# Opening of the first sequence: norm statistics from the transposed x

## The reference, cut to what matters

```python
mod = jnp.dot(jax.nn.silu(c), w_ada) + b_ada
shift1, scale1, gate1, shift2, scale2, gate2 = [m[:, None, :] for m in jnp.split(mod, N_MOD, axis=-1)]

h = (_rmsnorm(x, g_mix) * (1.0 + scale1) + shift1).astype(dt)   # x * rsqrt(mean(x*x, -1) + EPS) * g
proj = jnp.einsum('bsd,de->bse', h, w_in)
q, k, v, g_sw, p, gate_a, gate_b = jnp.split(proj, IN_SPLITS, axis=-1)
...
log_g_f = jax.nn.log_sigmoid(ret_decay_f.astype(jnp.float32))   # decay constants of the retention
log_g_b = jax.nn.log_sigmoid(ret_decay_b.astype(jnp.float32))
```

## Time and profile before

| | |
|---|---|
| median of 3 runs | 2575.28 us (2574.32 to 2575.88) |
| the profiled execution's own time | 2576.01 us |
| its span, first to last instruction | 2574.2 us |
| TensorE busy | 2517.1 us, 98% |
| VectorE, ScalarE, POOL busy | 71%, 46%, 68% |
| read from HBM | 284.36 MB |

### The profile page before, as it was taken

How to read it: one execution, slowest core, us unless ns; L and a number is a source line. 1 busy time by engine, 2 the same in 40 slices (tenths; PEclk the granted TensorE clock), 3 DMA queues, 4 the chain that set the end, 5 groups by cost and what they waited for, 6 DMA issues and landing times.

```text
span 2574.2 us, 34798 instructions
## 1 busy us (share of the span) xinstructions
PE 2517.1 (98%) x12684; PEld 2106.4 (82%) x12684; DVE 1820.2 (71%) x2182; ACT 1176.8 (46%) x1818; POOL 1741.0 (68%) x1165
## 2 busy tenths in 40 slices
PE   6999999999999999999999999999999999999998
PEld 3889898978778888878888888888777888888886
DVE  4978888877886666765859797978678555555434
ACT  5433333335654545555634333333456554555443
POOL 1777777757287777655656969696655877775545
PEclk9999999999999999999999999999999999999998
DMA  9124242446055355497631424241541323325764
GB/s 332 42 84 136 84 136 84 152 178 211 25 164 177 129 172 172 160 347 226 191 117 42 158 62 156 64 157 52 187 123 53 115 86 115 107 88 193 210 193 147
DMA packets 296009, 362.15 MB, mean 141 GB/s; under 512 B 17312, under 2 KB 178464, under 8 KB 295840
## 3 DMA queue, kind: packets, MB, share of 16 engines
q1 hardware_dynamic: 292960, 349.44, 42.0%
q10 hardware_dynamic: 2880, 10.49, 1.1%
HBM read 284.36 MB, written 75.50 MB: 140 GB/s over the span
## 4 chain that ended last, share of the span: by engine, by line
PE 82%; DVE 10%; ACT 2%; issue 2%; DMA 1%; POOL 1%; SPq 1%; DVEq 0%; POOLq 0%; ACTq 0%
PE ps L1099 27%; PE ps L1265 15%; PE ps L1529 13%; PE ps L1461 9%; PE ps L1160 5%; PE ps L1480 3%; PE ps L1370 3%; DVE state L2890 1%; PE ps L1548 1%; PE ps L1583 1%; DVE qdT L2871 1%; PE ps L1197 1%; PE ps L1314 1%; PE ps L1559 1%; DVE late_rows L2698 1%
## 5 line engine op out<-in xcount | busy, mean ns | idle before, releaser
L2276 POOL TENSOR_TENSOR f_w<-f_ring,f_w 128x512 fp32r<-128x512 f32 x434 | 595.3, 1378 | 397.2 <-ACT f_w L1857 392.2
L1099 PE MATMUL ps<-hc_hi,f_w 128*128 128x512 f32 x2240 | 690.4, 389 | 3.5 <-ACT u_act L1931 2.9
L2215 POOL TENSOR_TENSOR f_w<-f_ring,f_w 128x512 fp32r<-128x512 f32 x282 | 468.1, 1674 | 202.2 <-ACT f_w L1650 201.8
L1099 PEld LDWEIGHTS ps<-hc_hi,f_w 128*128 128x128 f32 x2240 | 420.0, 188 | 92.9 <-ACT u_act L1931 3.7
L1099 PE MATMUL ps<-hc_lo,f_w 128*128 128x512 f32 x1120 | 435.8, 389 | 0.0
L1265 PE MATMUL ps<-act_ring,f_w 128*128 128x512 f32 x1848 | 421.4, 390 | 2.7 <-ACT f_w L1857 1.4
L1265 PEld LDWEIGHTS ps<-act_ring,f_w 128*128 128x128 f32 x1848 | 346.5, 188 | 76.6 <-issue 3.2
L1857 ACT ACTIVATE f_w<-f_ring 128x512 fp32r<-128x512 f32 x434 | 269.8, 623 | 250.8 <-POOL f_ring L2286 109.5
L1529 PE MATMUL ps<-hb,f_w 128*128 128x512 f32 x1440 | 347.4, 395 | 0.0
L1650 ACT ACTIVATE f_w<-f_ring 128x512 fp32r<-128x512 f32 x282 | 176.0, 627 | 356.0 <-POOL f_ring L2223 186.7
L1529 PEld LDWEIGHTS ps<-hb,f_w 128*128 128x128 f32 x1440 | 268.3, 188 | 61.3 <-issue 6.7
(11 more groups left out here) (262 smaller groups left out, 4047.4 us busy)
## 6 DMA issues: line engine op xcount, KB each, us to landing
f_ring<-in_w_in SPq DMA_DIRECT2D x176, 256.0 KB, 4.3
f_ring<-in_w_up SPq DMA_DIRECT2D x160, 256.0 KB, 3.4
f_ring<-gated_out SPq DMA_DIRECT2D x154, 256.0 KB, 3.1
late_rows<-in_w_late SPq DMA_DIRECT2D x64, 512.0 KB, 4.6
gated_out<-gated_up SPq DMA_DIRECT2D x44, 512.0 KB, 4.2
f_ring<-down_sums SPq DMA_DIRECT2D x88, 256.0 KB, 3.0
gated_out<-t_gated SPq DMA_DIRECT2D x22, 768.0 KB, 6.1
f_ring<-in_w_down SPq DMA_DIRECT2D x66, 256.0 KB, 3.5
```

Of the source, the lines that this page charges most:

```text
L1099: ins = pe.matmul(ps_row[:, half_of(bank)], a[:, cols], b, start=i in (0, 1, 3) and k == 0 and n == 0, stop=k == KQ - 1 and n == 2, skip_g ...
L2215: pool.tensor_tensor(out[:, 1, :], raw, out[:, 0, :].bitcast(F32), ALU.subtract).then_inc(mix_lo.sem, 1)
L2276: pool.tensor_tensor(piece_slot(q)[:, 1, :], piece_raw(q), piece_slot(q)[:, 0, :].bitcast(F32), ALU.subtract).then_inc(piece_lo.sem, 1)
```

## The change

The natural x of the first sequence is no longer loaded. The squares are taken from the transposed x, in a new buffer `first_sq` at the address where the natural x was: for each half of the tokens ScalarE squares the eight chunks (`square_first`), VectorE adds the eight squares (`squares_of_first`, seven sums), TensorE adds over the partitions with four one-column matmuls (`statistics_of_first`), and VectorE adds epsilon on reading the sums (`mean_of_first`). From the power on, the way is the old one.

The transposed x is loaded as sixteen half chunks: the first token half by eight loads on ACT's queue, in place of four natural tiles; the second by eight loads on SP's queue (`later_half`), behind the first column half of the weights and four weight loads of `w_in`. The loads of the decay logits and of the constants behind the identity move behind these.

On TensorE the column sums of the first half stand behind product 3, and the spread behind product 5 instead of 4. After step 6 TensorE waits for the second half's sums; the spread of the second half stands after step 11 instead of 14; the products of the second column half stand in two groups of four, after steps 15 and 19.

On VectorE the decay constants stand behind the second `diagonal`, ahead of the scaling of piece 4; the last three operations on them stand behind the scaling of piece 9. On ScalarE the squares of the second half stand between and behind the modulations of pieces 2 and 3, and the exponentials around `row_factors(first, 1)`.

```diff
+        first_sq = at("first_sq", 128, [P, KC, HALF])
...
         @block.sync
+            sp.dma_start(vecT[:, :], vec).then_inc(vec_in, 16)
             sp.dma_start(cst[:, C_ID:C_ID + P], consts[:, C_ID:C_ID + P]).then_inc(const_in, 16)
-            sp.dma_start(vecT[:, :], vec).then_inc(vec_in, 16)
-            for half, src in enumerate((decay_f, decay_b)):
-                sp.dma_start(lg[:, half, :, :].rearrange("p a b -> p (a b)"), src.partition_broadcast(P)).then_inc(decay_in, 16)
-            sp.dma_start(cst[:, C_ID + P:C_ALL], consts[:, C_ID + P:C_ALL]).then_inc(decay_in, 16)
...
             for k in range(KQ, KC):
                 early_tile(0, k)
-            turned_chunk(0)
-            turned_chunk(1)
-            second_tile(4)
-            second_tile(5)
-            turned_chunk(2)
             for j in range(2, 4):
                 mix_in(mix0, j)
-            second_tile(6)
-            second_tile(7)
-            turned_chunk(3)
+            for k in range(KC):
+                later_half(k)
+            for half, src in enumerate((decay_f, decay_b)):
+                sp.dma_start(lg[:, half, :, :].rearrange("p a b -> p (a b)"), src.partition_broadcast(P)).then_inc(decay_in, 16)
+            sp.dma_start(cst[:, C_ID + P:C_ALL], consts[:, C_ID + P:C_ALL]).then_inc(decay_in, 16)
...
         @block.tensor
+            def statistics_of_first(half):
+                pe.wait_ge(*x_summed.at(first, (KC - 1) * (half + 1)))
+                if half:
+                    pe.wait_ge(*rrow_done.at(first, 1))
+                for t in range(4):
+                    col = (1 - half) * HALF + t
+                    ins = pe.matmul(ps[:, 3, col:col + 1], first_sq[:, 0, t * P:(t + 1) * P], ones[:, 0:1],
+                                    start=True, stop=True)
+                ins.then_inc(x_stat.sem, 1)
...
                 early_product(0, k)
-                if k == 4:
+                if k == 3:
+                    statistics_of_first(0)
+                if k == 5:
                     spread_rstd(first, (0,))
...
                 def of_first(n):
-                    if n == 14:
+                    if n == 6:
+                        statistics_of_first(1)
+                    if n == 11:
                         spread_rstd(first, (1,))
                     if n == 16:
                         pe.wait_ge(*rrow_done.at(first, 2))
-                    if n in range(12, 20):
-                        early_product(1, n - 12)
+                    if n in (15, 19):
+                        for k in range(n - 15, n - 11):
+                            early_product(1, k)
...
         @block.scalar
+            def square_first(half, k):
+                if half:
+                    act.wait_ge(*xt_in[k].at(first, 16))
+                    act.wait_ge(*x_stat.at(first, 1))
+                else:
+                    act.wait_ge(*x_in[k].at(first, 16))
+                act.activation(first_sq[:, k, :], xT[0][:, k, half_of(half)], ACT.Square,
+                               scale=D ** -0.5).then_inc(x_squared.sem, 1)
...
-            for t in range(TT // 2):
-                load_x(0, t)
+            for k in range(KC):
+                act.dma_start(xT[0][:, k, half_of(0)], xt[k * P:(k + 1) * P, half_of(0)]).then_inc(x_in[k].sem, 16)
...
             mix_high(mix0, 2)
             mix_high(mix0, 3)
-            square_x(first, 4)
+            square_first(1, 0)
+            square_first(1, 1)
             modulate_piece(first, 0, 0, 8, 2)
-            square_x(first, 5)
-            square_x(first, 6)
-            square_x(first, 7)
+            square_first(1, 2)
+            square_first(1, 3)
             modulate_piece(first, 0, 0, 8, 3)
+            for k in range(KQ, KC):
+                square_first(1, k)
+            act.wait_ge(table_step, 1)
+            act.activation(small[:, 1, :], small[:, 0, :], ACT.Exp, scale=-1.0).then_inc(table_act, 1)
             row_factors(first, 1)
+            act.wait_ge(table_args, 1)
+            act.activation(pairT[:, :, 0:T_GAIN], pairT[:, :, 0:T_GAIN], ACT.Exp).then_inc(table_act, 1)
...
         @block.vector
+            def squares_of_first(half, ks):
+                for k in ks:
+                    dve.wait_ge(*x_squared.at(first, KC * half + k + 1))
+                    if k > 1:
+                        dve.wait_ge(*x_summed.at(first, (KC - 1) * half + k - 1))
+                    dve.tensor_tensor(first_sq[:, 0, :], first_sq[:, 0, :], first_sq[:, k, :],
+                                      ALU.add).then_inc(x_summed.sem, 1)
...
             scale_first(2)
             norm_low(first, 0, 1)
+            squares_of_first(1, range(1, 3))
             scale_first(3)
             norm_low(first, 0, 2)
-            diagonal(first, (1,))
+            squares_of_first(1, range(3, 4))
             norm_low(first, 0, 3)
+            squares_of_first(1, range(4, KC))
+            mean_of_first(1)
+            diagonal(first, (1,))
+...
             dve.wait_ge(*rrow_done.at(first, 2))
             scale_first(4)
```

More of the change, by code:

```diff
@@ L2318, in _ @@
                 tiles = slice(4 * half, 4 * half + 4)
-                pool.wait_ge(*x_squared.at(first, 4 * half + 4))
-                pool.tensor_scalar(x_ms[:, tiles], x_ms[:, tiles], EPS, None, ALU.add).then_inc(x_eps.sem, 1)
                 pool.wait_ge(*x_eps.at(first, half + 1))
@@ L2433, in norm_scale @@
                 k, begin, end = pieces[where[0]][i]
-                dve.wait_ge(*xt_in[k].at(where, 16))
+                if where[0] == "first" and begin == 0:
+                    dve.wait_ge(*x_in[k].at(where, 16))
+                if where[0] == "swap" or end == S:
+                    dve.wait_ge(*xt_in[k].at(where, 16))
                 at_k = xT[seq][:, k, begin:end]
@@ L2643, in _ @@
-            step(dve.tensor_scalar(small[:, 0, :], logit, 0.0, None, ALU.min))
-            step(dve.scalar_tensor_tensor(logit, small[:, 5, :], -2.0, small[:, 0, :], ALU.mult, ALU.add))
-            for d in range(2):
-                pos = cst[:, C_POS + d:C_POS + d + 1]
-                dve.tensor_scalar(pairT[:, :, T_DK + d:T_DK + 4:2], lg[:, d, :, :], pos, None, ALU.mult)
-            for d in range(2):
-                half = slice(d * DK, (d + 1) * DK)
-                dve.tensor_scalar(pairT[half, :, T_DC:T_DC + 2], lg[half, d, :, :], float(P), None, ALU.mult)
@@ L2664, in _ @@
-            for col, row, factor in ((T_GAIN, R_GAIN, 0.25), (T_PS, R_PS, 0.5)):
-                step(dve.tensor_scalar(pairT[:, :, col:col + 2], vecT[:, row:row + 8].rearrange("p (a b) -> p a b", b=2),
-                                       factor, None, ALU.mult))
+            def squares_of_first(half, ks):
[5 more added lines that the diff above has]
+                                      ALU.add).then_inc(x_summed.sem, 1)
@@ L2668, in copy_ada, with mean_of_first @@
+            def mean_of_first(half):
+                dve.wait_ge(*x_stat.at(first, half + 1))
+                col = (1 - half) * HALF
+                dve.tensor_scalar(x_ms[:, 4 * half:4 * half + 4], ps[:, 3, col:col + 4], EPS,
+                                  None, ALU.add).then_inc(x_eps.sem, 1)
+            squares_of_first(0, range(1, KC))
+            mean_of_first(0)
+            diagonal(first, (0,))
             def copy_ada(part):
@@ new lines, in _ @@
+            dve.wait_ge(table_act, 1)
+            step(dve.tensor_scalar(small[:, 2, :], small[:, 1, :], 2.0, None, ALU.add))
+            step(dve.reciprocal(small[:, 2, :], small[:, 2, :]))
+            step(dve.tensor_tensor(small[:, 3, :], small[:, 1, :], small[:, 2, :], ALU.mult))
+            step(dve.tensor_tensor(small[:, 4, :], small[:, 3, :], small[:, 3, :], ALU.mult))
+            step(dve.tensor_scalar(small[:, 5, :], small[:, 4, :], 1.0 / 17, None, ALU.mult))
+            for k in range(7, 0, -1):
+                step(dve.scalar_tensor_tensor(small[:, 5, :], small[:, 5, :], 1.0 / (2 * k + 1), small[:, 4, :],
+                                              ALU.add, ALU.mult))
@@ new lines, in _ @@
+            step(dve.scalar_tensor_tensor(small[:, 5, :], small[:, 5, :], 1.0, small[:, 3, :], ALU.add, ALU.mult))
+            step(dve.tensor_scalar(small[:, 0, :], logit, 0.0, None, ALU.min))
+            step(dve.scalar_tensor_tensor(logit, small[:, 5, :], -2.0, small[:, 0, :], ALU.mult, ALU.add))
+            for d in range(2):
+                pos = cst[:, C_POS + d:C_POS + d + 1]
+                dve.tensor_scalar(pairT[:, :, T_DK + d:T_DK + 4:2], lg[:, d, :, :], pos, None, ALU.mult)
+            for d in range(2):
+                half = slice(d * DK, (d + 1) * DK)
+                dve.tensor_scalar(pairT[half, :, T_DC:T_DC + 2], lg[half, d, :, :], float(P), None, ALU.mult)
@@ L2739, in _ @@
+            for h in range(2):
+                half = slice(h * DK, (h + 1) * DK)
+                for d in range(2):
```

(4 more changed lines are left out.)

61 lines of the change are left out of this document (18 added, 43 removed).

## The result

The changed kernel takes 2584.8 us (median of 7 runs, 2582.13 to 2585.53), the kernel before 2575.92 (7 runs beside them): ratio 1.003, 95% interval 1.002 to 1.0039. It is slower by 8.9 us, where 3.4 were forecast. The profiled run took 2584.82 us with a span of 2583.0.

What follows compares the result with a forecast made beforehand. TensorE, busy 98% of the span, bounds the kernel, so step 23's start decides: 24.5 (T) + 33.4 (path) + 1.8 (half clock) = 59.7 against 56.27, 3.4 us later, giving 2578.7 us; range 2572.5 to 2582.

Steps and rivals of the forecast that it cites:

- the first half of the statistics: Opening: eight ScalarE squares, seven VectorE sums, column sums and the later spread were to hide behind the weight tiles' loading.
- the 1.35 us pace of the tiles: Opening, DMA engines full: one 512 KB weight tile feeds one TensorE product every 1.35 us, 1.08 busy and 0.27 idle.
- T: Start of ScalarE's first modulation, 26.93 us before; forecast 24.5, bounds 22.5 and 26.9.
- the tail from tile to T as before: Opening: the time from the last weight tile's landing to ScalarE's first modulation was taken as unchanged.
- a faster clock: Opening: if TensorE's clock rises sooner, T is near 23.5 instead of 24.8; 24.5 was taken.
- The lull: DMA engines at 211 instead of 394 GB/s from 5 to 9 us; removing it was to bring 1.86 us.
- loads bring nothing: Rival: T stays near 26.9; step 23 +4.0 us, or +5.8 with the clock fallen, 2581.1 us; chance 0.19.
- step 23: Step of three q/k/v matmuls starting TensorE's unbroken run, at 56.27 us before; forecast 59.7, 3.4 later, carried to the end.
- The wait behind step 6: TensorE stops until the second half's sums of squares are done: a new idle of 4.7 us.
- the constants took 5.13 us (5.1): VectorE's decay constants, no longer under cover, put 5.1 us between second diagonal and scaling of piece 4.
- The clock fell to half behind that wait: TensorE at half clock after the new wait: twelve matmuls lose 2.4 to 2.5 us, 1.8 counted, bounds 0 and 2.5.
- step 17: Step of three q/k/v matmuls, 47.67 us before; forecast T + 25.1, VectorE last by 0.6 us, plus 1.8 for the clock.

Runs made afterwards that it cites:

- the split constants: Kernel before with constants' loads later, their VectorE work split over its waits, turned chunks and weights ahead of second natural tiles, products grouped; two versions: 2575.14 and 2574.21 us.
- the first of the two last versions: Kernel before with constants' loads behind turned chunk 0, their work split, chunks 1 and 2 and weights 2 and 3 read earlier, products grouped: 2575.14 us, 0.9993.

## Why the prediction was wrong

The step that failed is the first half of the statistics: "Both hide behind the 1.35 us pace of the tiles, for which I keep T as above." T was forecast at 24.5 and is 27.46. Of the 3.0 us, 1.6 are the longer way from the last tile to T (5.03 us, where 3.43 were kept "with the tail from tile to T as before"). Another 1.0 us is a term that was mis-sized: the last tile was to land up to 2.1 us earlier and landed 1.07 earlier. The other 0.3 had been taken off T for a faster clock.

- The loads. The lull is gone, but from 5 to 9 us they ran at 361 GB/s and not at the 394 counted on, and from 1 to 5 us at 224 where the kernel before had 258. That is 0.27 MB, or 0.7 of the missing 1.0 us (an estimate from these rates). In the other runs of these loads the gain was 1.2 to 2.3 us, so the rest may be chance; with natural x and the later constants it was 2.3.
- TensorE had no room for the statistics. At half clock a product takes 1.08 of the 1.35 us between tiles. From the end of the fourth product (16.77) to the end of the last (25.72) lie 8.95 us: four products of 1.0, 4.1; column sums 1.7; the spread 2.0; 0.9 of waiting for the diagonal, 0.2 for a tile. I priced the work by the engines that feed TensorE, and of TensorE itself asked only whether tiles were late. The row was there: three products back to back in 2.25 us in front of the copy mean that tiles had already been waiting for TensorE (by their landings 1.7, 0.8 and 0.3 us).
- The column sums cost twice what the rows of the middle of the kernel gave: 1.05 at full clock, 1.87 here. And VectorE's sums ended 0.7 us before the fourth product did, not 3.
- The diagonal took 1.75 us beside POOL, 0.69 with POOL held back. I had priced it by 0.69 rows in which POOL did nothing. The Trainium skill (SBUF — State Buffer, section on the two separate sides) says that a VectorE instruction with two SBUF inputs and a GpSimd one that reads SBUF lock the shared port pair for a whole instruction, and the later one waits in full. The trace agrees in the main: POOL's piece ran from 19.90 to 21.17, the diagonal, begun at 19.97, ended 0.55 us behind it, and POOL's next piece took 1.71 us instead of 1.27. This is the largest part: with POOL held back the way from the last tile to T is 2.80 to 3.34 us, no longer than before, although column sums and spread stand where the change put them.

```profile
21.13 1.71 POOL L2229 TENSOR_TENSOR f_w<-f_ring,f_w 128x512 fp32r<-128x512 f32 x1
```

So the outcome is the rival "loads bring nothing" in its number for T (26.9, clock fallen, +5.8; here +7.0 at step 23) and not in its mechanism: the loads brought 1.1 us, and the way behind them took 1.6 more.

What was right:

- The wait behind step 6: 4.7 forecast, 4.58 measured, ended by VectorE's sum. The diagonal ended at T + 17.1 (16.9), the constants took 5.13 us (5.1).
- The clock fell to half behind that wait (0.50 from 41.5 to 48.3 us), as was forecast and as the page of the Trainium skill that the prediction names says. With the wait filled it stayed up, and with the squares cut too. The fall cost 2.75 us on fifteen matmuls (2.4 to 2.5 on twelve was the estimate); of this the path lost at least 1.4 by the run with the wait filled, 1.8 were forecast.
- Behind step 23 the delay was carried on, up to 2280 us.
- One detail was not right: with the clock down TensorE is last at step 17 (55.05, without a wait in front of it), and its spread (48.66) releases the scaling of piece 4 0.8 us behind the constants. That VectorE is last there holds at the full clock only, as with the wait filled.

Left open: what makes TensorE's waits near the end, where the last 1.8 us come from, and how much of the scatter of the last tile's landing (21.25 to 22.43 with the same loads) is chance in the order of packets of the two queues. Beside the later experiments the kernel before took 2576.66 to 2577.40 us (medians of 15 to 27 runs), up to 1.5 more than in the seven runs beside the change. The changed kernel was not timed beside those, so the 8.9 us may be a little high; step 23 shows 7.0.

## What to carry to other kernels

When work is moved into the order of an engine that waits for loads, add up that engine's own busy time at the clock it has there; a wait in front of each piece is room only for what is shorter than it. A wait that is added to TensorE can cost more than its length: here 3.2 us, and 3.2 more of TensorE's time in half-clock matmuls, of which filling the wait gave the path 1.4 back. So the place for late work is in waits that other engines have anyway, as the split constants show. When T moves with chance in the loads, split it at the landing of the last tile. Price an operation of VectorE by a row in which POOL runs beside it, if POOL will.

## What the runs showed of the hardware

- The granted-clock column has no record before 34.7 us in the profile of after and shows 1.00 there by default, while twelve matmuls took 5.24 us; in the opening the clock is read from the matmuls' spacing.
- VectorE's small operations can stretch beside POOL as the large ones do: with POOL's low pieces running, a 128x16 product of the constants took 0.92 us instead of 0.17 (at 30.99 in the first of the two last versions), and an addition of squares 1.56 instead of 0.69 (at 32.50 in the changed kernel).
- Idle matmuls between the first products kept the full clock until 19.3 us; then it was half for 3.4 us, although TensorE had waited no longer than 0.72 us at a time since 14.9.
- The granted clock can fall behind a shorter wait, and hold behind a longer one: it was half from 42.7 us in the run with the column sums behind step 12, whose wait of 1.17 us ended at 40.33, and full to 100 us and beyond in the run with the squares cut, whose wait of 1.38 us ended at 37.12.
